# Convolution taps, decayed keys and output units moved in a gated delta rule layer

## The reference

```python
qkv, z_a, a_lg, b_lg, cf_val, cf_glu, z_b, gate_lg = jnp.split(proj, pts, axis=-1)
qkv = jax.nn.silu(depthwise_conv_centred(qkv, qkv_conv_w))          # 5 taps
o = gated_delta_chunked(forward) + flip(gated_delta_chunked(backward))
o = o * lax.rsqrt(jnp.mean(o * o, axis=-1, keepdims=True) + EPS) * dn_norm_w
y_a = (o * jax.nn.silu(z_a)) @ w_dn_out
u = depthwise_conv_centred(cf_val * jax.nn.sigmoid(cf_glu), cf_conv_w) + cf_conv_b   # 31 taps
u = jax.nn.silu(layer_norm(u, cf_ln_w, cf_ln_b))
y_b = (u * jax.nn.silu(z_b)) @ w_cf_out
y = (gate[:, :, 0] * y_a + gate[:, :, 1] * y_b) @ w_out
```

## Time and profile before

| | |
|---|---|
| median of 3 runs | 2220.59 us (2220.25 to 2221.42) |
| the profiled execution | 2214.12 us |
| its span, first to last instruction | 2212.8 us |
| PE busy | 2079.3 us, 94% |
| DVE busy | 1269.6 us, 57% |
| ACT busy | 873.2 us, 39% |
| POOL busy | 894.4 us, 40% |
| mean granted clock of PE | 0.98 |

### The profile page before, as it was taken

How to read it: one execution, slowest core, us unless ns; L and a number is a source line. 1 busy time by engine, 2 the same in 40 slices (tenths; PEclk the granted TensorE clock), 3 DMA queues, 4 the chain that set the end, 5 groups by cost and what they waited for, 6 DMA issues and landing times.

```text
span 2212.8 us, 26550 instructions
## 1 busy us (share of the span) xinstructions
PE 2079.3 (94%) x10668; PEld 1661.1 (75%) x10668; DVE 1269.6 (57%) x1943; ACT 873.2 (39%) x1404; POOL 894.4 (40%) x431
## 2 busy tenths in 40 slices
PE   7999999998999999999999899799999999799997
PEld 5888787775666788888787677678788777688785
DVE  5422224747767533222225999887543999887443
ACT  4222233223444542222235376343533375343532
POOL 4444443332113344444444553343344554343342
PEclk9999999999999999999999999999999999999999
DMA  4333332321101233333332222100232222001232
GB/s 151 108 133 95 96 95 88 113 69 37 29 30 58 73 99 95 96 96 96 95 95 76 67 77 69 36 30 20 77 96 88 87 83 67 29 30 29 76 96 76
DMA packets 46185, 169.08 MB, mean 76 GB/s; under 512 B 5232, under 2 KB 6000, under 8 KB 45808
## 3 DMA queue, kind: packets, MB, share of 16 engines
q1 hardware_dynamic: 45344, 165.60, 23.9%
q10 hardware_dynamic: 720, 1.79, 0.2%
HBM read 165.27 MB, written 2.10 MB: 76 GB/s over the span
## 4 chain that ended last, share of the span: by engine, by line
PE 73%; DVE 19%; ACT 6%; issue 2%; DMA 1%; POOL 0%; ACTq 0%; DVEq 0%
PE ps L381 20%; PE ps L383 20%; PE ps L382 20%; DVE cu L1744 3%; PE ps L408 2%; DVE blk_t L1846 1%; DVE outer L1844 1%; PE ps L574 1%; PE ps L590 1%; DVE acc L1871 1%; PE ps L559 1%; PE ps L861 1%; PE ps L818 1%; DVE rt L1727 1%; ACT dl L1356 1%
## 5 line engine op out<-in xcount | busy, mean ns | idle before, releaser
L2060 POOL TENSOR_TENSOR wlo<-raw,whi 128x1024 fp32r<-128x1024 f32 x300 | 737.6, 2465 | 930.7 <-ACT whi L939 930.1
L381 PE MATMUL ps<-xh,whi 128*128 128x512 f32 x1600 | 652.0, 407 | 29.3 <-POOL wlo L2060 16.7
L383 PE MATMUL ps<-xh,wlo 128*128 128x512 f32 x1600 | 627.2, 392 | 0.0
L382 PE MATMUL ps<-xl,whi 128*128 128x512 f32 x1600 | 626.9, 392 | 0.0
L381 PEld LDWEIGHTS ps<-xh,whi 128*128 128x128 f32 x1600 | 302.9, 189 | 116.5 <-issue 28.8
L939 ACT CAST whi<-raw 128x1024 fp32r<-128x1024 f32 x300 | 312.5, 1044 | 180.8 <-DMA raw<-in_stream 180.7
L383 PEld LDWEIGHTS ps<-xh,wlo 128*128 128x128 f32 x1600 | 302.4, 189 | 65.1
L382 PEld LDWEIGHTS ps<-xl,whi 128*128 128x128 f32 x1600 | 303.2, 190 | 63.2 <-issue 5.6
L1744 DVE SCALAR_TENSOR_TENSOR cu<-up,lcols,cu 128x512 f32<-128x512 f32 x180 | 188.4, 1089 | 0.1
L1470 DVE TENSOR_TENSOR ml<-mid,mh 128x512 fp32r<-128x512 f32 x42 | 60.1, 1435 | 164.1 <-ACT mh L995 164.1
L2096 POOL TENSOR_TENSOR cu<-cu,prod 128x512 f32<-128x512 f32 x60 | 87.2, 1454 | 155.0 <-ACT prod L1165 153.8
(11 more groups left out here) (342 smaller groups left out, 3038.2 us busy)
## 6 DMA issues: line engine op xcount, KB each, us to landing
raw<-in_stream SPq DMA_DIRECT2D x300, 512.0 KB, 3.6
w1k<-in_w SPq DMA_DIRECT2D x1, 2048.0 KB, 8.4
w1v<-in_w SPq DMA_DIRECT2D x1, 2048.0 KB, 10.1
outT<-h SPq DMA_DIRECT2D x4, 512.0 KB, 2.7
h<-in_xT ACTq DMA_DIRECT2D x2, 512.0 KB, 7.3
h<-in_xT SPq DMA_DIRECT2D x2, 512.0 KB, 7.6
mats<-in_mats ACTq DMA_DIRECT2D x1, 448.0 KB, 10.3
msk<-in_masks SPq DMA_DIRECT2D x1, 258.0 KB, 3.8
```

Source lines behind the costliest of these rows:

```text
L381: pe.matmul(out, wh, hi, start=first, stop=False)
L382: pe.matmul(out, wh, lo, start=False, stop=False)
L383: return pe.matmul(out, wl, hi, start=False, stop=last)
L2060: pool.tensor_tensor(m.wlo[:, slot, :], m.raw[:, slot, :], m.whi[:, slot, :].bitcast(F32), ALU.subtract).then_inc(s.wlo)
```

## The change

- In `decayed_keys`' place, the keys come directly behind `U`, and the point's taps behind them.
- `POINT_TAPS`: one tap fewer at "decay" and at "level1", two more at "keys". The sum stays 14 a chunk.
- `tap_plan`: the groups of the GLU stage have 1, 2, 4 and 2 taps behind them where they had 1, 2, 10 and 7, and `QKV_PHASE_TAPS` goes, with one tap each in eight steps. So 84 taps are left for the delta rule instead of 65; with 56 done at the points, 28 stand behind the last chunk instead of 9.
- The output stage: the stream has the z units of `o` first. Their Silus go into eight buffers (`z_o`, `z_cu`) in place that the delta rule no longer needs. PE does two z units, the sums of `o`, two z units, the mean, two z units, the variance and two z units; ACT and DVE follow that order. The squares of the convolution branch go to `rt`, and its mean to PSUM bank 5. DVE scales `o` before it centres the convolution branch.
- The merge takes the half of `o` first.

```diff
-POINT_TAPS = {"decay": 2, "level1": 2, "join1": 2, "level2": 1, "join2": 2, "last": 1, "keys": 2, "out": 2}
+POINT_TAPS = {"decay": 1, "level1": 1, "join1": 2, "level2": 1, "join2": 2, "last": 1, "keys": 4, "out": 2}
...
-    for c, n in enumerate((1, 2, 10, 7)):
+    for c, n in enumerate((1, 2, 4, 2)):
...
-QKV_PHASE_TAPS = [LATER_TAPS[j:j + 1] if j < 8 else [] for j in range(12)]
-DELTA_TAPS = LATER_TAPS[8:]
+DELTA_TAPS = LATER_TAPS
...
         z_unit(0)
-        pe.wait_ge(s.conv, 3 * l + 3)
-        pe.wait_ge(s.shared, 30 * l + 30)
-        sum_rows(ps[:, 4, :], [m.cu[:, c, :] for c in range(4)]).then_inc(s.mean)
         z_unit(1)
         for c in range(4):
             pe.wait_ge(s.o_sq, 4 * l + c + 1)
             sum_rows(ps[:, c, :], [m.rt[:, c, :]]).then_inc(s.o_sums)
+        z_unit(2)
+        z_unit(3)
+        pe.wait_ge(s.conv, 3 * l + 3)
+        pe.wait_ge(s.shared, 30 * l + 30)
+        sum_rows(ps[:, 5, :], [m.cu[:, c, :] for c in range(4)]).then_inc(s.mean)
+        z_unit(4)
+        z_unit(5)
         pe.wait_ge(s.cu_sq, 4 * l + 4)
-        sum_rows(ps[:, 5, :], [m.dl[:, 0, c, :] for c in range(4)]).then_inc(s.var)
-        for n in range(2, 8):
-            z_unit(n)
+        sum_rows(ps[:, 5, :], [m.rt[:, c, :] for c in range(4)]).then_inc(s.var)
+        z_unit(6)
+        z_unit(7)
...
-            act.activation(m.prod[:, n % 2, :], ps[:, Z_BANKS[n % 3], :], ACT.Silu).then_inc(s.filled)
+            z = m.z_o if n < 4 else m.z_cu
+            act.activation(z[:, n % 4, :], ps[:, Z_BANKS[n % 3], :], ACT.Silu).then_inc(s.filled)
...
+        act.activation(ps[:, 5, :], ps[:, 5, :], ACT.Exp, scale=-0.5).then_inc(s.root_cu)
+        z_unit(6)
         for c in range(4):
...
+            act.wait_ge(s.cu_n, 4 * l + c + 1)
+            act.activation(m.cu[:, c, :], m.cu[:, c, :], ACT.Silu, bias=lcl(m, l, "ln_b", c),
+                           scale=lcl(m, l, "ln_w", c)).then_inc(s.cu_silu)
+        z_unit(7)
         weights_upto(u0 + L_OUT + AHEAD + 1)
-        split_rows(3)
+        for k in range(4, 8):
+            split_rows(k)
...
-            for ch, k in QKV_PHASE_TAPS[j]:
-                cf_tap(ch, k)
...
+        for n in range(4, 8):
+            times_z(n)
+            if n > 4:
+                low_part(n - 1)
+        low_part(7)
...
                 if lv == 1:
-                    conv("decay")
                     if i:
                         decayed_keys(l, i)
+                    conv("decay")
...
-        units += [pairs(proj(glu), proj(val)), proj(qkv)[QKV_ORDER], gates, proj(zb), proj(za),
+        units += [pairs(proj(glu), proj(val)), proj(qkv)[QKV_ORDER], gates, proj(za), proj(zb),
```

More of the change, by code:

```diff
@@ L158 @@
     "outer": (221824, [P, 256], F32),
+    "z_o": (158336, [P, 4, S], F32),
+    "z_cu": (215680, [P, 4, S], F32),
     "fh": (141952, [P, 8, S], F32R),
@@ L168 @@
     "pt0 pt1 ptc turned o_new pv cw cturn vcc gts cscore ysum mix_lo h_new yl up wab_lo ab qconv ab_raw ab_t "
[L169 to L174, removed]
+    "sq_qkv ab_read decay sums_qkv gl l2 cum d_kk kk_read picked d_pre d_min filled o_sq o_sums conv shared "
+    "mean cu_sq var o_dn d_snew d_vns d_onew d_t d_u d_att d_ys d_qd d_at d_y d_qk d_us d_uy d_ttk d_ttv d_kd "
+    "d_s0 d_ks d_rest d_vn d_s d_q d_o act_step raw0 raw1 raw2 raw3 whi in_h0 in_h1 in_h2 in_h3 xh square root "
+    "scaled2 sil angle trig mid mh poly tanh gts_sig negmax csub cexp mix_hi gate_scaled sg yh prod glu_sig y "
+    "nh zero qkv root_qkv soft_dve soft_act cum_s d_dec cum_d z_used o_root cu_c root_cu cu_n cu_silu d_vt eps "
+    "dve_step rms in_pos h_scaled d_t0 h_out out_dma "
 )
@@ L655, in merge @@
             pe.wait_ge(s.wlo, u0 + c + 1)
-            for r in (0, 1) if mixer else (1, 0):
+            for r in range(2):
                 for k in range(4):
                     if c == 0:
-                        pe.wait_ge(s.mix_lo, 8 * g + 4 * (r if mixer else 1 - r) + k + 1)
+                        pe.wait_ge(s.mix_lo, 8 * g + 4 * r + k + 1)
                     ins = multiply(u0 + c, 4 * r + k, ps[:, bank + r, :], fh[:, 4 * r + k, :], fl[:, 4 * r + k, :],
@@ L1272, in z_unit, with split_rows @@
             act.wait_ge(s.unit, u + 1)
-            if n >= 2:
-                act.wait_ge(s.z_used, 8 * l + n - 1)
-            act.activation(m.prod[:, n % 2, :], ps[:, Z_BANKS[n % 3], :], ACT.Silu).then_inc(s.filled)
+            z = m.z_o if n < 4 else m.z_cu
+            act.activation(z[:, n % 4, :], ps[:, Z_BANKS[n % 3], :], ACT.Silu).then_inc(s.filled)
+        def split_rows(k):
+            src = m.o[:, k, :] if k < 4 else m.cu[:, k - 4, :]
+            act.wait_ge(s.z_used, 8 * l + k + 1)
+            act.copy(m.fh[:, k, :], src).then_inc(s.mix_hi)
         weights_upto(u0 + L_Z + AHEAD + 1)
@@ L1281, in layer @@
             act.activation(m.rt[:, c, :], m.o[:, c, :], ACT.Square).then_inc(s.o_sq)
-        weights_upto(u0 + L_Z + 1 + AHEAD + 1)
+        z_unit(0)
+        z_unit(1)
+        for c in range(4):
+            act.wait_ge(s.o_sums, 4 * l + c + 1)
+            then(act.activation(ps[:, c, :], ps[:, c, :], ACT.Ln, bias=eps, scale=1.0 / P))
+        for c in range(4):
+            act.activation(ps[:, c, :], ps[:, c, :], ACT.Exp, scale=-0.5).then_inc(s.o_root)
+        z_unit(2)
+        z_unit(3)
@@ L1283, in layer @@
+        weights_upto(u0 + L_Z + 4 + AHEAD + 1)
         for c in range(4):
             act.wait_ge(s.cu_c, 4 * l + c + 1)
[L1285 to L1289, removed]
+            act.activation(m.rt[:, c, :], m.cu[:, c, :], ACT.Square).then_inc(s.cu_sq)
@@ L1290, in layer @@
+        z_unit(4)
+        z_unit(5)
+        for k in range(4):
+            split_rows(k)
+        weights_upto(u0 + L_Z + 6 + AHEAD + 1)
         act.wait_ge(s.var, l + 1)
         then(act.activation(ps[:, 5, :], ps[:, 5, :], ACT.Ln, bias=eps, scale=1.0 / (4 * P)))
+        act.activation(ps[:, 5, :], ps[:, 5, :], ACT.Exp, scale=-0.5).then_inc(s.root_cu)
+        z_unit(6)
         for c in range(4):
-            act.activation(ps[:, c, :], ps[:, c, :], ACT.Exp, scale=-0.5).then_inc(s.o_root)
@@ L1904, in layer @@
         delta(l, cf_tap)
[L1905 to L1909, removed]
         for c in range(4):
@@ L1913, in layer, with times_z, low_part @@
                                      op0=ALU.mult, op1=ALU.mult).then_inc(s.o_dn)
+        def times_z(n):
+            dst, z = (m.o[:, n, :], m.z_o[:, n, :]) if n < 4 else (m.cu[:, n - 4, :], m.z_cu[:, n - 4, :])
+            dve.wait_ge(s.filled, 24 * l + GATE_UNITS + n + 1)
+            if n < 4:
+                dve.wait_ge(s.o_dn, 4 * l + n + 1)
+            else:
+                dve.wait_ge(s.cu_silu, 4 * l + n - 3)
+            dve.tensor_tensor(dst, dst, z, ALU.mult).then_inc(s.z_used)
+        def low_part(n):
+            src = m.o[:, n, :] if n < 4 else m.cu[:, n - 4, :]
+            dve.wait_ge(s.mix_hi, 8 * l + 8 + n + 1)
+            dve.wait_ge(s.z_used, 8 * l + n + 1)
+            dve.tensor_tensor(m.fl[:, n, :], src, m.fh[:, n, :].bitcast(F32), ALU.subtract).then_inc(s.mix_lo)
+        dve.wait_ge(s.conv, 3 * l + 3)
+        dve.wait_ge(s.mean, l + 1)
+        for c in range(4):
+            dve.scalar_tensor_tensor(out=m.cu[:, c, :], in0=ps[:, 5, :], scalar=-1.0 / (4 * P), in1=m.cu[:, c, :],
+                                     op0=ALU.mult, op1=ALU.add).then_inc(s.cu_c)
+        for n in range(4):
+            times_z(n)
+        for n in range(4):
+            low_part(n)
         dve.wait_ge(s.root_cu, l + 1)
```

1 line of the change is left out of this document (added).

## The result

The changed kernel took 2198.92 us in the median of four executions (2198.46 to 2202.93) beside 2220.79 (2220.25 to 2221.42) for the kernel before: ratio 0.9905, 95% interval 0.989 to 0.9921. The experiments showed that these four executions of before were long ones: 61 more spread from 2211.7 to 2225.4 with a median of 2216.8, and the granted clock fell from .982 to .975 as the time rose. The changed kernel, repeated beside eleven of them, took 2199.71 (2198.21 to 2202.26): ratio 0.9925 (0.9909 to 0.9942). So the gain is about 17 us (13 to 20 by that interval); most of the other five of the 21.9 are the long executions. A gain of 7.2 was forecast.

What follows compares the result with a forecast made beforehand. PE's work plus its pauses, almost all for VectorE, was taken to bound the kernel. Terms 5.1 + 5.3 - 3.2 = 7.2 us off the 2212.8 span gave 2205.6, plus 7.8 carried over 2213.4; range 2197 to 2220.

Steps and rivals of the forecast that it cites:

- the first rival: Delta rule: moved keys gain the whole 2.52 us a chunk and all four slow stretches go; 2197.8 us, chance 0.2.
- No idle before the first QKV square; 10.0 unchanged; mean without a wait.: Signs of a right forecast in PE's waits: QKV stage, pause before the delta rule's first chunk, output stage.
- Part A: GLU and QKV stages: moving 19 taps a layer out gains 4.5 us in layer 0, 0.6 in layer 1, 5.1 together.
- the eight taps of the QKV stage give nothing more: QKV stage: VectorE already waits 1.61 us for PE at unit 11, so removing these taps gains nothing.
- The sentence on the 10.0 us: Before the delta rule's first chunk: the block-inverse chain starts when PE ends unit 11, so the 10.0 us pause stays whole.
- Part B: Delta rule: keys directly behind the inverse gain 2.4 us over six chunks plus 2.9 of slow stretches, 5.3; bounds 0 and 20.9.
- slow stretches: Chunks 1 and 3 of each layer: 1.2 GHz PE clock behind a pause, 1.45 us each; two of four go, 2.9 us.
- Part C: Output stage and merge: taps hidden, merge waits 3.2 us against 1.6; loss 1.6 a layer, 3.2 us; bounds +3.2 and -6.
- I carry the difference over: Whole kernel: timed median 2220.59 lies 7.8 us above the profiled span 2212.8; 7.8 is added to 2205.6, giving 2213.4.
- Keys in full: Delta rule: VectorE's taps slip between GpSimd's instructions, second-level transposes are not late; 2197.8 us, chance 0.2.
- tap rival: Output stage: taps behind the rule run at 1.59 us, the mean is 12.1 late a layer; 2237.6 us, chance 0.08.
- table rival: Output stage: longer ScalarE table switches delay z unit 6, the merge waits 7.2 us more; 2220.6 us, chance 0.07.

Runs made afterwards that it cites:

- e2: Changed kernel with all 19 taps a layer back in the GLU and QKV stages; 2206.92 us, ratio to before 0.9961.
- e8: Changed kernel with ScalarE's four convolution row splits ahead of the last weight cast of the z units; 2193.65 us, ratio 0.9897.
- e1: Kernel before with only the decayed keys directly behind U and the new POINT_TAPS counts; 2205.65 us, ratio 0.9951.
- e12: Changed kernel with the eleven GLU taps put back, the eight QKV taps still moved; 2208.09 us, ratio 0.9954.
- e9: Changed kernel with the eight QKV taps put back, the eleven GLU taps still moved; 2206.63 us, ratio 0.9953.
- e4: Kernel before with only the new output stage and merge order, 9 taps behind the last chunk; 2219.39 us, ratio 1.0015.
- e5: The changed kernel again, unaltered, beside more executions of the kernel before on one chip; 2199.71 us, ratio 0.9925.
- e6: Changed kernel with no taps between keys and scores (decay 0, level1 0, keys 6); 2192.46 us, ratio 0.989.
- e3: Changed kernel with the old POINT_TAPS counts and the decay taps ahead of the decayed keys again; 2217.0 us, ratio 0.9987.
- e7: Changed kernel with the old tap counts (decay 2, level1 2, keys 2), keys still directly behind U; 2229.74 us, ratio 1.0055.

## Why the prediction was right and wrong

The direction and the places were right, and so were the mechanisms of parts B and C; the sum was too small by more than half, 7.2 of some 17 us. That 2198.9 lies in the range, 1.9 us above its lower end, is in part luck: the range reached so low only because it took in the first rival. Point by point:

- *No idle before the first QKV square; 10.0 unchanged; mean without a wait.* All three are in the profile.
- **Part A** (5.1 forecast): 8.4 by the windows, 10.0 by e2 at equal clock. Layer 0 came near, 5.6 (161.4 against the 155.8 of e8) for 4.5. Two steps failed. The first is the size of layer 1, 0.6 for 2.3 by the windows and 3.6 by those of e2: it counted one wait, though the trace of before has more in that stage, which are gone in the changed kernel:

```profile
PE ps L700 <- ACT kk L1218: 0.3, 1, 0.3
PE ps L726 <- DVE qkv L1801: 0.2, 1, 0.2
```

And e1, whose code is the same there, waited 1.43 and 0.57 at the squares. The second is "the eight taps of the QKV stage give nothing more: at unit 11 VectorE waits 1.61 us for PE already". A wait of VectorE at unit 11 says nothing of what PE waits for ahead of that unit: with the eight taps beside the GLU taps there are these 0.3 and 0.2 us (e2; e12 has neither), and in e9 the 1.62 us for `pick_b`. They are worth 1.3 and 1.0 us beside the GLU taps (e2 against e12) and 2.0 and 1.8 without them (e9). The sentence on the 10.0 us is right (the pause keeps its length), but it begins earlier by all that is gained ahead of it.
- **Part B** (5.3): 9.7 by e1's windows of the delta rule against before (212.6 and 213.6 us), 11.2 in its median. The chain was right to a few tenths: from `U` to the end of the keys 1.2 us (1.3 forecast), to the end of tap one 2.1 (2.2), of tap two 4.8 (5.1), to the copy 8.15 (8.6). But a pause is the small difference of two long chains: 0.4 us on the copy and 0.25 in PE's own steps made a pause of 1.44 out of 2.1, and the pauses of a chunk shorter by 1.08 instead of 0.4. Of that 0.79 arrives, so the term was mis-sized, some 4.7 us over six chunks for 2.4. Of the slow stretches in the chunks all four went instead of two, at the prediction's price 5.8 for 2.9. The two make 10.5, a little over the 9.7 of the windows.
- **Part C** (-3.2): 2.4 us of waits a merge against 3.2, place and cause as forecast. Each merge is 2.5 us longer and each wait of 1.0 at the z units gone, a loss of some 3.0 in all; e4 gives -2.4 at equal clock. e8 shows that GpSimd's split makes the wait. A lower clock behind that pause, 1.2 us a merge in some executions (e5, e6), was not in the sum. The taps behind the rule took 0.95 us, not 1.06; they were hidden with 7 us to spare.
- **The base.** "I carry the difference over" took the 7.8 us between the profiled span and the three timed runs for a constant. Only 1.3 of it is one (span 2212.8, time 2214.12; in the changed kernel 2198.1 and 2199.35). The other 6.5 are spread that goes with the clock: before has executions from 2211.7 at .981 to 2225.4 at .975, and the profiled one was a short one. The changed kernel has no pause over 1.5 us in chunks 1 to 3 and spreads under 5 us, so its profiled execution stands for its timed ones.
- **Rivals.** "Keys in full" gave nearly the measured time for a wrong reason: the transposes are late, by 1.44. Its slow stretches did all go. What is held by GpSimd in these traces is the tap, the scores' second product, the low part and `pick_b`, all with two SBUF inputs; the keys, with one input from PSUM, are not (0.6 each). The rule of the Trainium skill, page SBUF — State Buffer, section Who interferes with whom, which the prediction set against this rival, says the same, and the traces agree with it. The tap rival and the table rival fell. (The latter's 3.6 us a layer don't follow from its own numbers: 8.9 + 4.1 against 9.0 is 4.0.) The new loads look like this, on ACT between the variance and z unit 6:

```profile
1595.35 1.28 ACT L1312 ACT_TABLE_LOAD   x1
1596.64 0.58 ACT L1312 ACTIVATE ps<-ps 128x512 f32<-128x512 f32 x1
1597.24 1.28 ACT L1280 ACT_TABLE_LOAD   x1
```

A load takes 1.28 us and the next instruction follows 0.01 to 0.15 us behind it. The drain of 1.38 that the Trainium skill, page ScalarE: Activation LUTs, section What ACT_TABLE_LOAD costs, adds to each switch is not in this trace, and the measurement decides.

Open stays why e3, with the same pauses as before, is granted less clock than before (.976 against .980). That pauses of 3.1 us and more open the way to the lower clock in the chunks is shown by e1, e3, e7 and the changed kernel; what decides in a single execution is not.

## What to carry to other kernels

That an engine waits at one place does not make the instructions ahead of it free: before calling an edit free, look for every place ahead where another engine waits for its results, and for what a shifted instruction will then meet. Where long instructions of a helper engine hold short ones, as GpSimd's held the taps here, count each short one as one instruction of the helper; put instructions between them that are not held, here those that read PSUM, or move the held ones to a place where the engine waits anyway. And before a forecast is anchored to one profiled execution, look at its granted clock beside those of the timed ones.

## What the hardware showed

- Up to the third group of layer 0's GLU stage nothing differs between these kernels, yet the time to the end of the 5.4 us wait there ran from 1232.2 us (e9) to 1240.4 (e4) in the profiles, with more time at a granted clock of 0.50 in the longer ones.
- Taps and GpSimd's instructions took turns: four taps in a row took 7.12 us, 1.78 each, while GpSimd ran five instructions (e7); a tap with GpSimd idle took 0.74.
- Pauses of 1.44 us and less were followed by no granted clock of 0.50 in chunks 1 to 3 of any profile here; pauses of 3.1 us were in some chunks and not in others (before: four of six), those of 4.1 us in e7 in all six.
